# Twelve more projection chains beside the delta rule, weights split in halves, query rows loaded four slots ahead

## The reference

```python
h = rms_norm(x, norm_mix_g[l])
proj = h @ w_in[l]
(qa, ka, va, qi, ki, wi, qb, kb, vb, zb, bb, ab) = jnp.split(proj, SPLIT_POINTS, axis=-1)
...
qi = rope(qi.reshape(bsz, seq, IDX_HEADS, IDX_DIM), pos)      # index queries
ki = rope(ki.reshape(bsz, seq, 1, IDX_DIM), pos)[:, :, 0]     # index keys
...
o_a = sparse_indexer_attention(qa, ka, va, qi, ki, wi)        # top 256 keys of each query
o_b = gated_deltanet(qb, kb, vb, zb, bb, ab, conv_w[l], ...)  # conv, SiLU, chunkwise delta rule
x = x + jnp.concatenate([o_a, o_b], axis=-1) @ w_out[l]
h = rms_norm(x, norm_ffn_g[l])
x = x + jnp.square(jax.nn.relu(h @ w_ff1[l])) @ w_ff2[l]
```

## Time and profile before

| | us |
|---|---|
| median of 3 runs | 4060.3 |
| lowest and highest | 4058.37, 4064.96 |
| the profiled execution | 4064.05 |
| its span in the profile | 4062.3 |
| mean granted TensorE clock | 0.927 of full speed |

### The profile page before, as it was taken

The page is one execution under the profiler, slowest core; times in us unless marked ns, Lnnn a source line. Parts: engine busy times, 40 slices in busy tenths (PEclk is TensorE's granted clock), DMA queues, the critical chain, the costliest instruction groups (busy, mean ns, idle before and its releaser), DMA issues.

```text
span 4062.3 us, 47354 instructions
## 1 busy us (share of the span) xinstructions
PE 3480.5 (86%) x16994; PEld 2838.5 (70%) x16994; DVE 2084.2 (51%) x3582; ACT 2170.1 (53%) x3674; POOL 1331.6 (33%) x673
## 2 busy tenths in 40 slices
PE   6999937778886885677999889999888999988997
PEld 5888826667665673456777767787767878867886
DVE  4043116667675675535455556656548575533222
ACT  3122216565754554357868667777775954433222
POOL 3111113424234341323433433333323333333442
PEclk8999968889988998688999998999998999999999
DMA  4411142222223222332333333333333333342222
GB/s 168 180 73 68 68 149 56 71 91 56 91 72 109 76 72 74 98 102 81 111 107 99 119 120 103 103 121 102 117 118 108 109 97 112 96 132 79 96 98 73
DMA packets 316296, 403.32 MB, mean 99 GB/s; under 512 B 24976, under 2 KB 240144, under 8 KB 312208
## 3 DMA queue, kind: packets, MB, share of 16 engines
q1 hardware_dynamic: 313040, 378.28, 30.3%
q10 hardware_dynamic: 3024, 22.02, 1.3%
HBM read 325.33 MB, written 74.87 MB: 99 GB/s over the span
## 4 chain that ended last, share of the span: by engine, by line
PE 29%; ACT 15%; DVE 7%; issue 5%; POOL 2%; SPq 1%; DMA 1%; ACTq 0%; DVEq 0%; POOLq 0%
PE m_ps L1994 8%; PE m_ps L1996 8%; PE m_ps L1995 8%; ACT m_junk L1707 6%; ACT m_wh L1764 2%; PE m_ps L2088 2%; PE m_ps L2074 2%; ACT m_prob L1791 1%; ACT m_verdict L1709 1%; ACT m_trial L1713 1%; ACT m_phi L1780 1%; PE m_ps L2059 1%; PE m_ps L2060 1%; PE m_ps L2037 1%; ACT m_rl L1723 1%
## 5 line engine op out<-in xcount | busy, mean ns | idle before, releaser
L1652 POOL TENSOR_TENSOR m_wl<-m_raw,m_wh 128x1024 fp32r<-128x1024 f32 x288 | 718.0, 2493 | 1413.1 <-ACT m_wh L1764 1413.1
L1994 PE MATMUL m_ps<-m_ah,m_wh 128*128 128x512 f32 x1280 | 538.1, 420 | 67.1 <-DVE m_al L1853 39.0
L1995 PE MATMUL m_ps<-m_al,m_wh 128*128 128x512 f32 x1280 | 512.8, 401 | 0.0
L1996 PE MATMUL m_ps<-m_ah,m_wl 128*128 128x512 f32 x1280 | 512.5, 400 | 0.0
L1994 PE MATMUL m_ps<-m_th,m_wh 128*128 128x512 f32 x1024 | 428.7, 419 | 41.5 <-DVE m_tl L1833 25.1
L1996 PE MATMUL m_ps<-m_th,m_wl 128*128 128x512 f32 x1024 | 406.6, 397 | 0.0
L1995 PE MATMUL m_ps<-m_tl,m_wh 128*128 128x512 f32 x1024 | 405.4, 396 | 0.0
L1707 ACT ACTIVATE m_junk<-m_sc,m_trial 128x1152 int8<-128x1152 f32 (+7 forms) x248 | 401.6, 1619 | 1.3
L1764 ACT ACTIVATE m_wh<-m_raw 128x1024 fp32r<-128x1024 f32 x288 | 302.7, 1051 | 127.0 <-PE m_ps L1996 122.0
L1994 PEld LDWEIGHTS m_ps<-m_ah,m_wh 128*128 128x128 f32 x1280 | 248.3, 194 | 133.2 <-issue 29.1
L1831 DVE TENSOR_TENSOR m_rl<-m_rl 128x512 f32<-128x512 f32 x128 | 93.8, 733 | 415.6 <-ACT m_th L1727 415.3
(11 more groups left out here) (306 smaller groups left out, 7339.8 us busy)
## 6 DMA issues: line engine op xcount, KB each, us to landing
m_raw<-w_units SPq DMA_DIRECT2D x288, 512.0 KB, 3.6
m_vals<-valsT SPq DMA_DIRECT2D x256, 128.0 KB, 3.6
projT<-work ACTq DMA_DIRECT2D x12, 1024.0 KB, 3.9
g_qkvz<-projT SPq DMA_DIRECT2D x16, 768.0 KB, 5.7
p_raw<-w_proj SPq DMA_DIRECT2D x24, 512.0 KB, 4.5
wraw<-w_proj SPq DMA_DIRECT2D x21, 512.0 KB, 3.5
projT<-stage ACTq DMA_DIRECT2D x9, 1024.0 KB, 3.9
work<-xT SPq DMA_DIRECT2D x8, 1024.0 KB, 5.5
```

The costliest lines, as they stand in the source:

```text
L1652: nc.gpsimd.tensor_tensor(wl[:, n % 3, :], raw[:, n % 2, :], wh[:, n % 3, :].bitcast(fp32), ALU.subtract).then_inc(w_lo, 1)
L1994: nc.tensor.matmul(dst, hi, rh, start=first, stop=False)
L1995: nc.tensor.matmul(dst, hi, r_low, start=False, stop=False)
L1996: return nc.tensor.matmul(dst, lo, rh, start=False, stop=last)
```

## The change

1. **Index queries.** Of the four index query chunks only block 0 (tokens 0 to 511) stays in the first stage. The other 12 chains move to `ProjectionPlan`, which now has 36 chains. A kind carries its number of blocks, and the four one-block chunks stand between convolution chunks: small, conv 0, index, index, conv 1, conv 2, index, index, conv 3 and so on.
2. **The plan of the second stage.** Blocks come in the order 1, 2, 3, 0, so that queries are there before their tiles. Halves stand in f0, f1, f5 of even rounds and f0, f1, f3, f5 of odd ones, in seven slots of round 0 (8 to 20) and in every second slot of rounds 16 and 17. Round 0 has 7 halves (before 1), rounds 1 to 15 have 52 (before 45), rounds 16 and 17 have 13 (before 2).
3. **Weights by halves.** 72 loads of 256 KB through three buffers, 72 high and 72 low operations on 512 columns, instead of 24 of each at 1024. The input block is issued by ScalarE in two halves, nine slots ahead of the next block's first chain.
4. **Query rows.** `rotation` leaves four slots between the load and the first rotation (before: one). The load waits for the store of its block's index chains, where they are made in this stage.
5. **The gated output** moves from b12 to b8 of the next round, into one buffer instead of two, and its square no longer shares a buffer with `wT`.
6. The plan's last VectorE slot is 12 ahead of the end (before 2), so the scores of the last tiles stand about four slots earlier.

```diff
-    kinds = [("plain", c, 0) for c in range(C_CONV) if c not in LATER]
+    conv = [("conv", C_CONV + k, k, NB) for k in range(N_CONV)]
+    index = [("plain", C_QI + k, 0, 1) for k in range(C_QA - C_QI)]
+    kinds = [("plain", C_SMALL, 0, NB)] + conv[:1] + index[:2] + conv[1:3] + index[2:] + conv[3:]
...
-    HERE = ("f0", "f1", "f5")
+    HERE = (("f0", "f1", "f5"), ("f0", "f1", "f3", "f5"))
+    ENDS = list(range(8, 21, 2)) + list(range(STAGES * 16, STAGES * 18 - 3, 2))
+    PAUSE = 9
+    RAW = 3
...
+                high = max(slot - 4, halves[h - 4] if h >= 4 else 0)
+                low = max(slot - 2, high)
+                self.put("sp", max(slot - 9, lows[h - self.RAW] + 1 if h >= self.RAW else 0), "weights", h)
...
+        slot = max(slot, self.queries_at(j) + 1)
         self.put("sp", slot, ("load", j))
-        slot += 1
+        slot += 4
...
+                        if stored_chains:
+                            sp.wait_ge(p_stored, 16 * (max(stored_chains) + 1))
...
-                if s == "b12":
-                    dv("oz")
-                    ac("orn")
-                    if t >= 2:
-                        pool.wait_ge(stored[t % 2], 16 * (t // 2))
-                    step(nc.gpsimd.tensor_tensor(out_b[:, t % 2, :, :], B("osq"), B("oz"), ALU.mult))
+                if s == "b8" and t:
+                    gated(t - 1)
...
+            def project_high(h):
+                act.wait_ge(w_in[h % rest.RAW], 16 * (h // rest.RAW + 1))
+                if h >= 4:
+                    act.wait_ge(p_done, h - 3)
```

More of the change, by code:

```diff
@@ L228, in _ @@
                         act.wait_ge(stored[u], 16 * (c // 2))
-                for tb in range(NB):
+                for tb in range(blocks):
                     act.wait_ge(acc_done, chain_at[c, tb] + 1)
@@ L307 @@
 class ProjectionPlan:
-    HERE = ("f0", "f1", "f5")
+    HERE = (("f0", "f1", "f5"), ("f0", "f1", "f3", "f5"))
+    ENDS = list(range(8, 21, 2)) + list(range(STAGES * 16, STAGES * 18 - 3, 2))
+    PAUSE = 9
+    RAW = 3
     def __init__(self, S):
-        self.chains = [(b, c) for b in range(S // 512) for c in LATER]
-        self.n_of_block = len(LATER)
-        free = [STAGES * r + m for r in range(S // P + 2) for m, s in enumerate(ROUND)
-                if STAGES * r + m >= 20 and (s in self.HERE or r == 0)]
+        index, NB = tuple(range(C_QI, C_QA)), S // 512
+        self.blocks = list(range(1, NB)) + [0]
+        self.chains = [(b, c) for b in self.blocks for c in (index if b else ()) + LATER]
+        self.last_of_block = {b: max(n for n, x in enumerate(self.chains) if x[0] == b) for b in self.blocks}
+        self.chain_slot = {}
+        free = [STAGES * r + m for r in range(S // P + 2) for m, s in enumerate(ROUND)
+                if (s in self.HERE[r % 2] and 0 < r < S // P) or STAGES * r + m in self.ENDS]
+        halves = []
+        for n, (b, c) in enumerate(self.chains):
+            pause = self.PAUSE if n and self.chains[n - 1][0] != b else 1
+            for half in range(2):
+                halves.append(next(x for x in free if not halves or x >= halves[-1] + (1 if half else pause)))
@@ L318, in __init__ @@
         self.parts = {}
-        last_half = -3
-        for n in range(len(self.chains)):
-            a, z = free[2 * n], free[2 * n + 1]
-            assert a - last_half >= 1
+        lows = []
+        for n, (b, c) in enumerate(self.chains):
+            a, z = halves[2 * n], halves[2 * n + 1]
             for half, slot in enumerate((a, z)):
                 self.put("pe", slot, "half", n, half)
-            self.put("act", max(a - 3, last_half), "high", n)
-            self.put("pool", max(a - 3, last_half), "low", n)
-            self.put("act", z + 1, "evac", n)
-            self.put("sp", max(a - 8, 0) if n < 2 else max(a - 8, before + 1), "weights", n)
-            if n % self.n_of_block == 0:
-                self.put("sp", 12 if n == 0 else last_half + 1, "block", n // self.n_of_block)
-            self.put("sp", z + 1, "store", n)
-            before, last_half = a, z
+            for h, slot in ((2 * n, a), (2 * n + 1, z)):
+                high = max(slot - 4, halves[h - 4] if h >= 4 else 0)
+                low = max(slot - 2, high)
+                self.put("sp", max(slot - 9, lows[h - self.RAW] + 1 if h >= self.RAW else 0), "weights", h)
+                self.put("act", high, "high", h)
+                self.put("pool", low, "low", h)
+                lows.append(low)
+            self.put("act", z + 1, "evac", n)
+            if n == 0 or self.chains[n - 1][0] != b:
+                for half in range(2):
+                    self.put("act", 0 if n == 0 else halves[2 * n - 2 + half] + 1, "block", self.blocks.index(b), half)
+            self.put("sp", z + 2, "store", n)
+            self.chain_slot[b, c] = z + 2
@@ L365, in __init__ @@
         steps = lambda j: [] if j in self.late else ["begin"] + (["fix"] if j in self.on_act else ["probe"] * BITS) + ["value", "ties", "bias"]
+        last_slot = end - 12
         total = sum(sum(cost(j, k) for k in steps(j)) + 760 * len(pieces(j)) for j in self.tiles)
         slot = 16
-        rate = total / sum(SPARE[s % STAGES] for s in range(slot, end - 2))
+        rate = total / sum(SPARE[s % STAGES] for s in range(slot, last_slot))
         ahead = [0.0]
@@ L537, in deltanet_and_selection @@
         load = [sem(f"g_load{u}") for u in range(2)]
-        stored = [sem(f"g_stored{u}") for u in range(2)]
+        stored = sem("g_stored")
         done = {e: [sem(f"g_{e}_{part}") for part in ("front", "mid", "tail")] for e in ("pe", "dve", "act", "pool")}
@@ L656, in project_store, with store_tile @@
                 sp.dma_start(projT[c, :, 512 * b:512 * (b + 1)], p_out[:, :]).then_inc(p_stored, 16)
-            project = {"block": project_block, "weights": project_weights, "store": project_store}
+            def store_tile(t):
+                waits(sp, t, TAIL)[3]("out")
+                sp.dma_start(mixT[4:8, :, tokens(t)].rearrange("c p s -> p c s"), out_b[:, :, :]).then_inc(stored, 16)
+            project = {"weights": project_weights, "store": project_store}
             for r in range(NT + 2):
@@ L1023, in back @@
                     pe(name)
-                    if name == "wT" and t:
-                        waits(act, t - 1, TAIL)[3]("out")
                     step(nc.scalar.activation(B(name), bank(name), ACT.Copy))
@@ L1028, in back @@
                     pe("out")
+                    if t:
+                        waits(act, t - 1, TAIL)[3]("out")
                     step(nc.scalar.activation(B("osq"), bank("out"), ACT.Square))
```

135 lines of the change are left out of this document (76 added, 59 removed).

## The result

The changed kernel takes 3991.2 us, the median of 4 runs (3983.3 to 3996.1), against 4062.6 us for the kernel before, run beside it. The ratio is 0.982, with a 95% interval of 0.980 to 0.984. The profiled execution has a span of 3990.2 us, 72.1 us less than before, with a mean granted clock of 0.937 (before 0.927).

A forecast was written before the change was run, and what follows sets the result against it. TensorE was taken to bound the first stage and be nearest to a bound in the second, the third untouched. First stage -42 and second -20 (-50 + 15 + 21 - 10 + 4) gave -62 us: 3998 us, range 3957 to 4042.

The forecast's parts named there:

- the likeliest case: Whole kernel: the forecast itself, 3998 us, with 3975 to 4020 us given a chance of 0.53.
- First stage, -42: First stage: twelve chains fewer -65.3 us, two TensorE gaps +19.6, low clock behind them +4.
- Waits that go, -50: Second stage from round 1: TensorE waits ended by earlier query loads and the input block's move, -50 us, bounds 0 and -76.
- Extra halves in rounds 1 to 15, +15: Rounds 1 to 15: seven more halves, 19 us of TensorE, partly absorbed, +15 us, bounds 0 and +19.
- +4 for small parts: Second stage: 48 more, smaller weight splits; GpSimd grows 28 us and holds VectorE, +4 us; other small parts 0.
- A fifth is absorbed: Rounds 1 to 15: with TensorE 80% busy, a fifth of the added halves' 19 us hides, leaving +15 us.
- Rounds 16 and 17, +21: Last two rounds: eleven more halves, 30 us, fill half of 18.6 us idle time, +21 us (+11 to +30).
- Start and round 0, -10: Second stage's start: six more halves into 46.6 us idle, some 10 us held at weights; together -10 us (-25 to +10).
- (c): Second stage, rival: half-size weight loads hold ScalarE; at 1.2 us a half 4084 us, slower; chance 0.08.
- (b): Second stage, rival: query rows come as late as before, only block waits go; total -14, 4046 us; chance 0.17.
- (a): Second stage, rival: waits go entirely (-76 us) and halves hide; total -115, 3945 us, milder to 3960; chance 0.18.
- The signs: Profile: two 10 us first-stage gaps, table waits under 80 us, no 18 us or block wait, TensorE busy +65 or slightly less.

The follow-up runs named there:

- lead and end alone: Kernel before with only four slots instead of one from query load to rotation, and last VectorE slot 12 ahead of the end instead of 2: 3987.3 us.
- the run with the lead taken back: Changed kernel with one slot instead of four between the load of a tile's query rows and its first rotation: 4048.7 us, ratio 0.998.
- 24 halves light: Changed kernel with 11 of 12 matmuls left out of each of the moved chains' 24 halves, loads, splits and copies kept: 3992.3 us, ratio 0.984.

## Why the prediction was right, point by point

The time (3991 for 3998), the range, the sign and the likeliest case came out. Step by step:

**First stage, -42: right, with its reason.** Twelve chains, two gaps of 9.6 us, 4 us of low clock. The run with the index chunks last took exactly the last two away.

**Waits that go, -50: right in kind, too small, and put down to the wrong edits.** The term failed in two places. The working said that the scores of the last tile beginning earlier "helps VectorE, not TensorE", and priced that edit at nothing; alone it brings 33 us, 11 of them at the end and 12 in round 12, where tile 11's load moved ahead of the block in SyncE's order. It is also what makes the lead possible: the last scores need the slots. And 12 us were given to the block, which left SyncE's queue and is issued nine slots ahead; which queue issues it brings nothing, and the nine slots were not tried alone. Lead and end together brought 73 us on the kernel before (span of the profiled executions), with waits of 9.7 us for the block still in it; the upper bound of the term was 76. I had taken two thirds of the waits that TensorE shows. The lead's gain in round 0 (18 us) was in no term of mine.

**Extra halves in rounds 1 to 15, +15 and +4 for small parts: too dear.** Against the kernel with lead and end alone rounds 1 to 15 are 0 to 7 us longer. "A fifth is absorbed" fails as a rule: up to about 52 halves nearly all is absorbed, beyond that nothing. Busy share (80%) gave a price that holds on neither side of the corner. GpSimd's part was under-sized: the low parts take 100.7 us instead of 60.3, so 40 more and not 28, and a third of a microsecond comes through for each, not a seventh: 13 us where I had 4. It isn't to be seen apart, since it is within what the halves absorb or cost. ScalarE's high parts grew by the 20 us that I had (45.4 for 25.3), but the 1.65 us for each whole one that I made it from is no measured value: one takes 1.06 us before.

**Rounds 16 and 17, +21: right as a price of halves, and a part missing.** Between 76.6 us with lead and end alone and 100.9 here lie 24.3 us for ten halves more between the marks, 2.4 us each. The plan's end took 9 us off again.

**Start and round 0, -10: the sum near (-6), the working wrong.** I counted 10 us for ScalarE's wait at the weights; it is 15.5 and costs nothing. The gain of the lead (-18) and the change's cost here (+11, from 101.3 us with lead and end alone to 112.7) are both larger than what I had. What the block load does to the keys I named but didn't price.

**The rivals.** (c), ScalarE held at the weights, stayed away: 17.4 us of waits where I had set 20 as the sign, and none behind the first rounds. (b), query rows late as before, is the run with the lead taken back: 4049 us, where I had 4046; that this is so near is luck in part, since that run has the plan's end, which my sum priced at nothing. (a) had the waits about right (-76) and the middle nearer than the forecast had it (+12); it failed at the start and at the end.

**The signs.** The gaps, the tables, the longest wait and the block came as I said. TensorE's busy time in the second stage rose by 46 us (791 to 837), not by 65 or a little less: the clock in rounds 1 to 15 rose from 0.92 to 0.95 and gave back more than I had counted.

So errors of -23 us (waits), -12 to -19 (middle), +21 (start and round 0, +11 where I had -10) and +3 (end) met in one sum, and that it came out within 10 us is in part luck. A forecast cut into stretches and then tried edit by edit shows this; the total alone would have confirmed terms that are wrong.

What the change comes to: lead and end bring 73 us. The moved chains, with all that goes with them, bring 42 us in the first stage, where two gaps take 23 from them, and cost about as much in the second: 24 in the last rounds, in which TensorE has little slack, 11 at the start and up to 7 in between. With the gaps closed the kernel takes 3962.2 us, and now the chains pay: 25 us below the kernel with lead and end alone.

## What to carry to other kernels

When an in-order engine waits for a load, count the slots of the plan between issue and use on every queue it passes, and see which other load is due in the same slot; three slots of lead were worth 40 to 57 us here, and which queue issued the large load nothing. The price of work added beside a dependent chain isn't a share of its time: find the corner by taking work away (free below) and adding some (full price above), and fill up to it. When a unit of work is moved away, look at its old place too, for what its absence uncovers: here two gaps, which cost 23 us until the chunks were put in another order.

## What the runs showed of the hardware that I had not expected

- The granted clock takes back part of what is taken off TensorE: with 24 halves light it fell from 0.85 to 0.65 in round 0 and from 0.95 to 0.93 in rounds 1 to 15.
- A VectorE addition on an eighth of its columns took 0.28 us in the median instead of 0.75, but 0.62 on average instead of 1.04: 58 of 209 stood behind a running GpSimd operation, the longest for 2.46 us in all. Shorter operands save their columns and not the standing behind GpSimd.
- A GpSimd operation on half the columns took 1.40 us instead of 2.51, 11% more for the same columns.
